# Per-token sums of squares in eight normalisations, and eight modulation chunks instead of twelve at the outset

## The reference, cut to what matters

```python
mod = silu(c) @ w_ada + b_ada                  # 9 vectors of 1024: shift, scale, gate, three times
u = rmsnorm(h, g1) * (1 + sc1) + sh1
h = h + 0.5 * gt1 * swiglu(u, w_ffn1_in, w_ffn1_out)          # inner width 2816
u = rmsnorm(h, g2) * (1 + sc2) + sh2
h = h + gt2 * token_mixing(u, ...)             # w_in, pooling and rotary attention branches, w_out
u = rmsnorm(h, g3) * (1 + sc3) + sh3
h = h + 0.5 * gt3 * swiglu(u, w_ffn2_in, w_ffn2_out)
x = rmsnorm(h, g_final)
for i in range(2):                             # second block, alpha = sqrt(2)
    m = short_conv_mixer(x) if i == 0 else dsa_mixer(x)
    x = layer_norm(alpha * x + m, ...)
    x = layer_norm(alpha * x + hier_moe(x, ...), ...)         # 64 experts
```

## Time and profile before

| | us |
|---|---|
| median of 3 runs | 3233.83 (3233.78 to 3237.36) |
| the profiled execution, its time | 3232.88 |
| its span in the trace | 3231.1 |
| PE busy | 2769.7 (86%) |
| DVE busy | 1131.4 (35%) |
| ACT busy | 732.7 (23%) |
| mean DMA rate | 183 GB/s |

### The profile page before, as it was taken

How to read it: one execution, slowest core, us unless ns; L and a number is a source line. 1 busy time by engine, 2 the same in 40 slices (tenths; PEclk the granted TensorE clock), 3 DMA queues, 4 the chain that set the end, 5 groups by cost and what they waited for, 6 DMA issues and landing times.

```text
span 3231.1 us, 50719 instructions
## 1 busy us (share of the span) xinstructions
PE 2769.7 (86%) x20736; PEld 2061.6 (64%) x20736; DVE 1131.4 (35%) x2189; ACT 732.7 (23%) x1272; POOL 108.8 (3%) x175
## 2 busy tenths in 40 slices
PE   4999988999889998996787777879978867877787
PEld 3888863755568886884566666744446655666665
DVE  6655442122432244444311111228276442111113
ACT  2222321053232233222100000112265220000003
POOL 0000001000000000000000000000000000000000
PEclk7999999999999999997899999999899979999999
DMA  8455431111213322221299999741100108999990
GB/s 281 154 172 177 145 119 52 65 57 61 78 52 104 104 87 83 78 91 39 98 422 422 422 422 422 283 154 56 52 1 27 78 1 336 422 422 422 422 392 27
DMA packets 205500, 590.02 MB, mean 183 GB/s; under 512 B 9264, under 2 KB 133360, under 8 KB 156000
## 3 DMA queue, kind: packets, MB, share of 16 engines
q1 hardware_dynamic: 202304, 573.38, 46.2%
q0 software_dynamic: 2288, 12.39, 1.2%
q10 hardware_dynamic: 816, 2.99, 0.3%
HBM read 586.58 MB, written 7.38 MB: 184 GB/s over the span
## 4 chain that ended last, share of the span: by engine, by line
PE 67%; DMA 20%; DVE 8%; ACT 2%; issue 2%; SPq 1%; POOL 0%; ACTq 0%; DVEq 0%
PE bank L1520 32%; DMA ring<-in_exp_w 20%; PE bank L1787 8%; PE bank L1862 4%; PE bank L1641 3%; PE bank L1612 3%; PE bank L1761 2%; PE bank L1847 2%; PE bank L1513 2%; PE bank L1601 1%; PE bank L1509 1%; SPq L436 1%; PE bank L1689 1%; ACT U L659 1%; DVE rstd L995 1%
## 5 line engine op out<-in xcount | busy, mean ns | idle before, releaser
L1520 PE MATMUL bank<-parts 128*128 128x512 f32 x3008 | 937.5, 393 | 49.4 <-DVE parts L968 49.4
L1520 PEld LDWEIGHTS bank<-parts 128*128 128x128 f32 x3008 | 567.7, 190 | 171.3 <-issue 50.7
L1787 PE MATMUL bank<-ring,arena 128*64 128x256 f32 x4096 | 494.8, 392 | 179.8 <-DMA ring<-in_exp_w 179.2
L1520 PE MATMUL bank<-parts,ring_low 128*128 128x512 f32 x1504 | 589.1, 392 | 0.0
L1787 PEld LDWEIGHTS bank<-ring,arena 128*64 128x64 f32 x4096 | 326.8, 135 | 311.2 <-issue 202.8
L1520 PEld LDWEIGHTS bank<-parts,ring_low 128*128 128x128 f32 x1504 | 285.0, 189 | 59.6
L962 DVE TENSOR_TENSOR ring_low<-ring,parts 128x2048 fp32r<-128x2048 f32 x96 | 215.1, 2246 | 214.3 <-ACT parts L622 214.0
L1805 PEld LDWEIGHTS bank<-arena,ring 128*64 128x64 f32 x8192 | 265.8, 138 | 16.8 <-ACT arena L604 1.1
L1323 DVE SCALAR_TENSOR_TENSOR arena<-arena,bank 128x128 f32<-128x128 f32 x128 | 44.2, 346 | 655.5 <-ACT arena L732 655.5
L1805 PE MATMUL bank<-arena,ring 128*64 128x64 f32 x8192 | 263.1, 222 | 0.7 <-ACT arena L604 0.7
L604 ACT ACTIVATE arena<-bank 128x128 f32<-128x128 f32 (+2 forms) x228 | 92.2, 406 | 691.8 <-PE bank L1794 247.4
(11 more groups left out here) (273 smaller groups left out, 2361.2 us busy)
## 6 DMA issues: line engine op xcount, KB each, us to landing
ring<-in_exp_w SPq DMA_DIRECT2D x384, 1024.0 KB, 10.3
ring<-in_w_ffn_in SPq DMA_DIRECT2D x44, 1024.0 KB, 6.5
ring<-in_w_ada SPq DMA_DIRECT2D x36, 1024.0 KB, 5.4
ring<-in_w_ffn_out SPq DMA_DIRECT2D x20, 1024.0 KB, 5.1
ring<-in_w_in SPq DMA_DIRECT2D x18, 1024.0 KB, 5.0
ring<-in_conv_w_in SPq DMA_DIRECT2D x12, 1024.0 KB, 5.1
ring<-in_attn_w_in SPq DMA_DIRECT2D x10, 1024.0 KB, 10.0
ring<-in_attn_w_out SPq DMA_DIRECT2D x8, 1024.0 KB, 5.1
```

The source lines that it names most:

```text
L1520: i = mm(o, a[:, cols[0], cols[1]], b, start=first_ and n == 0, stop=last_ and n == 2)
L1787: x = mm(bank[s][64 * f:64 * f + 64, 0:2 * P].rearrange("p (w n) -> p w n", w=2), XW[:, s, k], ring[:, 3 * s:3 * s + 2, c0:c0 + 2 * P - 1: ...
```

## The change: what it does

**Sums per token.** The squared tile becomes the stationary operand in four 128x128 blocks and a single column of ones the moving one (`sums`): bank 0 receives four columns, token by partition. Root and reciprocal are taken of 128x4 values. DVE multiplies the identity by each of the four columns (`diag`), and four matmuls of ones with these (`rstd`) spread the result over the partitions of bank 6, from where DVE reads it. A root of one column (`small[:, 56:57]`) stands ahead of the squares. In normalisations 1 to 3 the squares of the first four tiles are made within the output projection, DVE adds them to one (`presum`), and PE sums that tile and the fifth within the projection's last chunk. For normalisation 0 ACT squares the input as it came, token by partition, with its accumulator.

**Order around it.** The last chunk of an output projection runs output by output, and DVE adds each to `H` as it is done; the first half is added within `out_low`. The layer norm's mean follows tile by tile. In the split normalisations ACT writes the high part straight from the multiplied tile, DVE the rest between its multiplications, and the first a and b products (the first two of the convolution) alternate tile by tile. The mixer's first chunk does the same with each tile of `U`.

**Modulation.** Eight chunks stand at the head; the odd ones are multiplied on PE with silu(c) as a moving column (`ada_columns`). 24 remain in the first SwiGLU, four move between the mixer's chunks. The gates are made after the first SwiGLU's loop.

**Loads.** The positions are loaded first on POOL, and the router's rows after the second `ffn_a`; the mixer's constants wait for the first output projection instead of `H`. The angles are made within the first output projection (`angles` in `out_low`, ahead of its third chunk). The sparse attention's semaphores are shared with the mixer's, with offsets.

The diff's core:

```diff
-ADA_FIRST = 12
+ADA_FIRST = 8
+ADA_FFN = 32
 ADA_ALL = 36
...
+                used = ("ada_mm", a + 1) if a < ADA_FIRST and a % 2 else ("ada_step", steps_before(a) + 8)
...
+        def steps_before(a):
+
+            return 8 * (a // 2) if isinstance(a, int) and a < ADA_FIRST else a * 8 - 8 * (ADA_FIRST // 2)
...
+            if 2 <= c < 2 + ADA_ALL - ADA_FFN:
+                ada_chunks(1)
...
+            pool.dma_start(posi, A["positions"][0].partition_broadcast(P)).then_inc(sem("rows"), 16)
+            pool.wait_ge(sem("ffn_a"), 2)
...
-            pool.wait_ge(sem("h"), 8)
+            pool.wait_ge(sem("ffn0_out_used"), 12)
...
+            act.wait_ge(sem("x_in"), 16)
+            for t in range(TT):
+                st.did(A_(U[:, 2 * t:2 * t + 2], xtok[:, t].rearrange("p (a b) -> p a b", a=2), ACT.Square,
+                          accum_out=small[:, 60 + t:61 + t]))
...
+                    if q == n // 2 + 1 and norm_no is not None:
+                        squares(norm_no, 0, range(4))
...
+                    else:
+                        act.wait_ge(sem("h"), 8 * (i - 1) + k + 1)
...
+                A_(small[:, 56:57], epsc[:, 0:1], ACT.Sqrt)
                 if i:
-                    act.wait_ge(sem("normed"), 8 * i)
-                A_(rstd[:], bank[7][:], ACT.Sqrt, scale=1.0 / D,
+                    squares(i, ln, range(KT) if ln else range(4, KT))
+                    act.wait_ge(sem("sumsq"), i)
+                A_(small[:, 48:52], bank[0][:, 0:4] if i else small[:, 60:64], ACT.Sqrt, scale=1.0 / D,
                    bias=epsc[:, 1:2] if ln else epsc[:, 0:1]).then_inc(sem("root"), 1)
+                if i == 0:
+                    weights_high(0)
+                    weights_high(1)
...
                     if split:
-                        act.wait_ge(sem("u"), 8 * i + k + 1)
-                        tile_high(UP[0][:, k], U[:, k])
+                        A_(UP[0][:, k], U[:, k], ACT.Identity, bias=shift(k)).then_inc(sem("t_high"), 1)
+                    else:
+                        A_(U[:, k], U[:, k], ACT.Identity, bias=shift(k)).then_inc(sem("u"), 1)
...
+                    if q == 2 and idle:
+                        idle()
+                    if q == n // 2 + 1:
+                        first_half()
...
+                    if presum is not None and q == min(n // 2 + 2, n - 1):
+                        dve.wait_ge(sem("squares"), 8 * presum - 4)
+                        st.did(TTn(U[:, 0], U[:, 0], U[:, 1], ALU.add))
+                        st.did(TTn(U[:, 2], U[:, 2], U[:, 3], ALU.add))
+                        st.wait()
+                        TTn(U[:, 0], U[:, 0], U[:, 2], ALU.add).then_inc(sem("presum"), 1)
+
+            def roots(i):
+                dve.wait_ge(sem("root"), i + 1)
+                seq(nc.vector.reciprocal(small[:, 52:56], small[:, 48:52]))
+                for t in range(TT):
+                    TSc(diag[:, t], ident, small[:, 52 + t:53 + t], None, ALU.mult).then_inc(sem("diag"), 1)
...
+                if i:
+                    roots(i)
+                dve.wait_ge(sem("rstd"), i + 1)
...
+                def rest(k):
+                    dve.wait_ge(sem("t_high"), tiles_at[parts_of] + k + 1)
+                    high_part = UP[0][:, k].bitcast(F32)
+                    if shift is None:
+                        i = TTn(UP[1][:, k], U[:, k], high_part, ALU.subtract)
+                    else:
+                        i = STT(out=UP[1][:, k], in0=U[:, k], scalar=shift(k), in1=high_part,
+                                op0=ALU.add, op1=ALU.subtract)
+                    i.then_inc(sem("t_low"), 1)
+
                 for k in range(KT):
-                    STT(out=U[:, k], in0=H[:, k], scalar=gain(k), in1=rstd[:],
+                    STT(out=U[:, k], in0=H[:, k], scalar=gain(k), in1=bank[6][:],
                         op0=ALU.mult, op1=ALU.mult).then_inc(sem("normed"), 1)
+                    if parts_of and k:
+                        rest(k - 1)
+                if parts_of:
+                    rest(KT - 1)
...
+            def bank_ready(name, n, half, d):
+                if half and d < 3:
+                    dve.wait_ge(sem("out_bank"), 3 * OUTS.index(name) + d + 1)
+                else:
                     dve.wait_ge(sem(name + "_used"), n * (half + 1))
-                    for d in range(4):
-                        k = 4 * half + d
-                        STT(out=H[:, k], in0=bank[k][:], scalar=gates[:, gate + k:gate + k + 1], in1=H[:, k],
-                            op0=ALU.mult, op1=ALU.add).then_inc(sem("h"), 1)
+
+            def gated_add(name, n, gate, half):
+
+                for d in range(4):
+                    k = 4 * half + d
+                    bank_ready(name, n, half, d)
+                    STT(out=H[:, k], in0=bank[k][:], scalar=gates[:, gate + k:gate + k + 1], in1=H[:, k],
+                        op0=ALU.mult, op1=ALU.add).then_inc(sem("h"), 1)
...
+            for a in range(0, ADA_FIRST, 2):
+                ada(a, a, a // 2)
+                for done in (a - 2, a - 1) if a else ():
+                    ada_mod(done, done)
+                if a == 4:
+                    dve.wait_ge(sem("keep"), 16)
+                    roots(0)
+            for done in (ADA_FIRST - 2, ADA_FIRST - 1):
+                ada_mod(done, done)
+            dve.wait_ge(sem("ada_mod"), ADA_FIRST)
+            modulated_gains(0)
...
+                if r % 2 == 0 and r // 2 <= ADA_ALL - ADA_FFN:
+                    a = ADA_FFN + r // 2
+                    if a < ADA_ALL:
+                        ada(mix_at[2 + r // 2] + 1, a, a, buf=AC_MIX)
+                    if a > ADA_FFN:
+                        ada_mod(a - 1, a - 1, 6)
...
+            def ada_columns(a):
+                landed(pe, "a", a)
+                if a >= 2:
+                    pe.wait_ge(sem("ada_mod"), a - 1)
+                w = chunk("a", a)
+                for j in range(2):
+                    for k in range(KT):
+                        x = mm(bank[4 + a % 2][:, P * j:P * j + 1], w[:, k, P * j:P * j + P], csil[:, k:k + 1],
+                               start=(k == 0), stop=(k == KT - 1))
+                x.then_inc(sem("ada_mm"), 1)
+
+            def sums(i, k, first_, ready, n):
+
+                pe.wait_ge(sem(ready), n)
+                for t in range(TT):
+                    x = mm(bank[0][:, t:t + 1], U[:, k, P * t:P * t + P], ones[:, 0:1],
+                           start=(first_ and t == 0), stop=(k == KT - 1 and t == TT - 1))
+                if k == KT - 1:
...
+
+            def rstd(i):
+                for t in range(TT):
+                    pe.wait_ge(sem("diag"), TT * i + t + 1)
+                    x = mm(bank[6][:, P * t:P * t + P], ones[:], diag[:, t], start=True, stop=True)
...
             def norm(i, ln):
                 if ln:
-                    pe.wait_ge(sem("h"), 8 * (i))
                     for k in range(KT):
-                        x = mm(bank[6][:], ones[:], H[:, k], start=(k == 0), stop=(k == KT - 1))
+                        pe.wait_ge(sem("h"), 8 * (i - 1) + max(k + 1, 4))
+                        x = mm(bank[2][:], ones[:], H[:, k], start=(k == 0), stop=(k == KT - 1))
                     x.then_inc(sem("mean"), 1)
-                for k in range(KT):
-                    pe.wait_ge(sem("squares"), 8 * i + k + 1)
-                    x = mm(bank[7][:], ones[:], U[:, k], start=(k == 0), stop=(k == KT - 1))
-                x.then_inc(sem("sumsq"), 1)
+                for k in range(KT) if ln else range(5, KT):
+                    sums(i, k, k == 0, "squares", 8 * (i - 1) + k + 1)
+                rstd(i)
+
+            pe.wait_ge(sem("csil"), 1)
+            for a in range(0, ADA_FIRST, 2):
+                ada(a, a, half=a // 2)
+                ada_columns(a + 1)
+                if a == 2:
+                    pe.wait_ge(sem("x_in"), 16)
+                    pe.wait_ge(sem("keep"), 16)
+                    for k in range(KT):
+                        if k >= 4:
+                            pe.wait_ge(sem("x_h"), k - 3)
+                        for t in range(TT):
+                            i = tp(bank[k % 4][:, P * t:P * t + P], xtok[:, t, P * k:P * k + P], ident)
+                        i.then_inc(sem("x_tp"), 1)
+                if a == 4:
+                    rstd(0)
 
...
+                        if it is None and r == s == 0:
+                            for k in range(KT):
+                                pe.wait_ge(sem("t_low"), tiles_at[f"ffn{i}"] + k + 1)
+                                for which, sm in enumerate((a, b)):
+                                    x = passes(bank[which][:], both(s0 + which), (k, slice(0, P)),
+                                               (UP[0][:, k], UP[1][:, k]), k == 0, k == KT - 1)
+                                    if k == KT - 1:
+                                        x.then_inc(sm, 1)
...
+                    for c in range(n):
```

(86 more changed lines are left out.)

278 lines of the change are left out of this document (112 added, 166 removed).

## The result

The changed kernel takes 3176.93 us (median of 4, 3175.45 to 3177.86), the kernel before 3234.51 (median of 4, 3233.78 to 3237.36): ratio 0.982, interval 0.9803 to 0.9837. It is faster by 58. The forecast was a gain of 93 and a time of 3140, and the measured time lies above the high end of its range, 3172. The profiled execution took 3177.06, 55.8 less than that of before, and its span, 3175.3, is shorter by the same 55.8.

What follows compares the result with a forecast made beforehand. PE held 67% and DMA 20% of the chain, with gaps where PE waits for normalisations. Gains 28.4 + 16.7 + 14.9 + 13.8 + 19.0 = 92.8 off 3232.9 gave 3140; range 3127 to 3172.

Steps and rivals of the forecast that it cites:

- outset: Start of the kernel up to the first product: at 53.9 in place of 82.28, a gain of 28.4.
- norm 1 and mixer: Norm 1's gap gains 19.7, the mixer's clock 1, four chunks moved into the mixer cost 4: net 16.7.
- behind it: the four layer norms and the stages between: Norms 4 to 7: gaps of 23.8, gaining 6.5 each in 4 and 6, 3.0 each in 5 and 7, together 19.0.
- The price of the new small matmuls: Single-column matmuls in sums and outset: 0.113 a record, 0.226 a float32 matmul, so 7.2 for a layer norm's sums.
- sums over 9: Sign in the layer norms: the forecast is wrong if their sums, priced at 7.2, take over 9.
- Rival A: Clock falls under single columns: first product at 65, layer norms +3 sums and +1 spreading, norms 1 to 3 +1; 3170; chance 0.30.
- The wait for the root: Outset: DVE waits for norm 0's root until 37.2 with chunk 6 queued behind; PE waits 1.3 for that.
- Norms 2 and 3: Gaps after the first and second SwiGLU shrink to 7.0, with 1.8 within the projections: gains 14.9 and 13.8.
- B: Adds within the projections make PE wait, up to 5 in each of five projections: 3165; chance 0.06.
- C: Outset bound by DMA or slots: first product at 66 instead of 54, time 3152; chance 0.07.
- D: Single-column matmuls do not overlap the next weight load: gain gone at 0.30 a record, 3335 at 0.5; chance 0.03.
- E: A wait left in place, positions or all eight tiles of `U`, still ends last: norm 1 keeps 15, 3155; chance 0.04.

Runs made afterwards that it cites:

- experiment 5: Changed kernel with 128 moving columns in place of one in both the normalisation sums and the outset's column chunks: 3139.94 us, ratio 0.971.
- experiment 1: Changed kernel with 128 moving columns of ones in place of one in the normalisation sums: 3150.27 us, ratio 0.9737.
- experiment 2: Changed kernel with silu(c) repeated over 128 moving columns in the outset's column chunks: 3166.82 us, ratio 0.9789.
- experiments 3: Changed kernel with all eight outset chunks on DVE and no column matmuls on PE: 3167.06 us, ratio 0.9789.
- experiment 7: experiment 5 with DVE making the first SwiGLU weight's low part before the last chunk's bias: 3140.16 us, ratio 0.9706.

## Why the prediction was wrong by 37

Gains in us, each the step from one start of the chain to the next: the first product, the mixer's output projection (836.43 before, 803.39, 791.27 in experiment 5), the first product behind norms 2 and 3, the end of the span (3138.1 in experiment 5):

| | forecast | changed kernel | experiment 5 |
|---|---|---|---|
| outset | 28.4 | 19.2 | 30.0 |
| norm 1 and mixer | 16.7 | 13.8 | 15.2 |
| norm 2 | 14.9 | 14.4 | 14.8 |
| norm 3, with the second SwiGLU | 13.8 | 14.6 | 14.8 |
| behind it: the four layer norms and the stages between | 19.0 | -6.2 | 18.2 |
| sum | 92.8 | 55.8 | 93.0 |

Of the 25.2 missing in the last part, 23.4 are the layer norms' sums and spreading (next paragraph). Another 0.6 is in the rest of their gaps: 30.4, 30.2, 28.7 and 29.9, together 119.2, for 4 x 23.8 = 95.2. The last 1.2 lies in the stages between them.

**The price of the new small matmuls is the step that failed.** The prediction took 0.226 for a float32 matmul with one column from the router's 72-column records and carried it to stretches where nothing but such matmuls runs. The price is right at the full clock: 3.63 for 32 records in the outset, 0.113 each. It is wrong where the granted clock is 0.50: there a record takes 0.22 and a matmul 0.44, and the clock fell to 0.50 while PE ran nothing but these single columns. In the layer norms the sums took 12.76, 12.43, 11.03 and 12.3, each for 7.2; that is 5.6, 5.2, 3.8 and 5.1 more. The spreading took 2.08 four times, where it takes 1.16 in experiment 1: 19.7 + 3.7, or 23.4 of the 37 that were missing. The prediction said what would show it wrong: sums over 9.

**Outset.** 9.2 of the miss. By the prediction's own steps: columns of 1 and 3 took 7.0 and 6.8 for 3.6, so the transposes began at 33.63 in place of 29.8, and took 6.4 for 5.4. DVE then waited for the root until 42.56 (37.2 in the forecast) with chunk 6 queued behind; that one's matmuls (2.05) and columns of 7 (6.83) were slow again. Rival A gave 65 for the first product; 63.09 came. The wait for the root, which the prediction named, is in all versions; where PE is fast it is shorter (5.06 in place of 8.60) and ends at 35.55 in experiment 2.

**Norm 1.** 18.7 (18.6 to 37.3 ahead) for 19.7; with 0.6 lost in the first SwiGLU and 4.3 in the mixer that is the table's 13.8. The 24 sums of the last three tiles, straight behind the products, took 2.73, or 0.114 each; the spreading took 2.08, at a granted clock of 0.50 (453 to 457). From the last product to the mixer's first are 7.2 (449.80 to 457.02) where the forecast had 6.3, so here A's +1 is what came. (Rows below: the changed kernel's timeline there; the first are a tile's sums between products of 512 columns.) The mixer's 4.3 (37.3 to 33.0) were forecast as 3. The prediction gave back 1 for the shorter gap ahead of its first 80 records, 36.64 before. That did not come: they took 16.71 + 20.60 = 37.3, and the granted clock stood at 0.50 in the first 5 us (457 to 462). In experiment 5, where the clock was 1.00 in the spreading, they take 15.67 + 20.60 = 36.3.

```profile
442.40 0.95 PE L1585 MATMUL bank<-ones,U 128*128 128x1 f32 x8
...
449.64 2.73 PE L1585 MATMUL bank<-ones,U 128*128 128x1 f32 x24
...
453.26 2.08 PE L1593 MATMUL bank<-diag,ones 128*128 128x128 f32 x8 [0.89 <-DVE diag L1021]
```

**Norms 2 and 3.** From the last product to the first behind the norm are 7.3 in both (850.84 to 858.13, 1222.91 to 1230.17) for 7.0. In gains: 14.4 for 14.9; norm 3 by itself 13.5 for 13.8, since 1.0 of the table's 14.6 is the SwiGLU's 1056 products, 241.42 for 242.46: inside the bounds of 2 that the prediction put on it. The chain behind norm 3's last product has one member that the forecast put elsewhere (start, us, engine and line):

```profile
1222.94 0.75 DVE H L1110
1223.69 2.20 DVE ring_low L986
...
1226.36 1.42 PE bank L1593 x8
```

DVE's rest of the second weight runs between the last add and the diagonals. Square, sums and root of the last tile take about as long beside it: the root ends at 1225.77, DVE's rest at 1225.89. So it costs 0.1; a faster sum would find it next.

**Layer norms, in all but the sums.** Mean, root, reciprocal, diagonals and shift came near the forecast: with the sums at the full clock a gap is 24.1 in experiment 1, and the last part gains 18.2 of 19.0 in experiment 5. The prediction's own terms for such a gap (7.15, 1.4, 7.2, 1.6, 5.4, 0.7) add up to 23.45 and not to 23.8; by them the forecast would have been 1.4 lower. One reading of it was wrong and without effect: the root's table load stood beside the sums in six of the eight normalisations before, not in seven. In norm 0 it came at 70.75, behind the sums (62.28 + 8.37), and the outset's reckoning counts it.

**Rivals.** A came. In the outset it was near in size and not in detail: A had PE's pieces double from chunk 3 on, those of 5 and 7 and the spreading among them; chunk 1's columns were slow too, and chunk 5's (3.63) and the spreading (1.14) were not. In the layer norms it came with more than it said: the clock had begun to fall in the stretch 1417 to 1420, so +5 where A had the later half double, +3. B did not: the sums and adds within the projections left PE's products at their pace, 114.52 for 504 of them in the output projection against 119.94 for 528, 0.227 each in both. C, D and E did not (experiments 3 and 2; no positions in the chain after norm 1).

A had a chance of 0.30 with the row at 0.50 for it and "loads end to end" against it. The argument against was the weak one: the row of before that kept the clock with loads end to end had 72 columns behind each load, and the loads were not shown to be what kept it. The Trainium skill, page "TensorE: Matmul & The Clock Gate", section "What's actually happening", says that activity releases the throttle. Experiment 1 agrees with it: it changed nothing but the columns behind each weight load, 1 to 128, and the granted clock then stayed at 1.00 in the layer norms' sums.

## What to carry to other kernels

Where a stretch of PE is bound by weight loads and stands by itself, give the matmuls a wider moving operand: 128 columns in place of one cost next to nothing at the full clock (0.116 a record for 0.113), and in the layer norms they kept it, 7.41 for 12.76. Price a small matmul at both levels of the clock, and ask of each stretch what ran just before it and whether the new work is of the kind that held the clock in some row; a row with the same weight loads is not yet such a row. When half of a job is moved to another engine, try the version in which it stays: here DVE alone would have done as well.

## What the runs showed of the hardware that was not expected

- Matmuls of one column, end to end without a pause, let the granted clock go from 1.00 (1413 to 1417) to 0.50 (1420 on), and in the outset the pace did not rise under them: two chunks of 32 took 6.99 and 6.83, where the second chunk with 128 columns took 3.74.
- Between products of 512 columns the same records keep their full pace: 0.95 for 8 at 442.40 in the changed kernel, behind output products at 0.227 each.
- A wide moving operand does not secure the clock by itself: behind a wait of 2.03 the last column chunk ran at 1.00 in experiment 5 (3.74) and began at 0.50 in experiment 7 (4.85).
- In the first 44 us of the changed kernel the listed granted clock reads 1.00 throughout, while 8 records of 128 columns took 2.04 at 12.85, 2.05 at 25.10 and 1.06 at 39.91. At the start of an execution the pace of the records is to be believed, not that column.
- One column with its load takes 0.113 a record and 128 columns 0.116 (7.41 / 64).
